# Two streamed attentions on one core: TensorE's products with V in halves around its waits, prompt scores and half of the sample scores further ahead in the second layer

## What is computed

```python
# first layer, 8 heads with two maps each
s = jnp.einsum('bqhcd,bkhcd->bhcqk', qb, kb).astype(jnp.float32) * scale
p = jax.nn.softmax(jnp.where(mask, s, -jnp.inf), axis=-1)
w = p[:, :, 0] - lam * p[:, :, 1]
outs.append(jnp.einsum('bhqk,bkhd->bqhd', w.astype(v.dtype), vb))
...
# second layer, 16 heads
z = jnp.einsum('bqhd,bkhd->bhqk', qb, kb).astype(jnp.float32) * scale
log_1m = jnp.where(mask, jax.nn.log_sigmoid(-z), 0.0)
suffix = lax.cumsum(log_1m, axis=3, reverse=True) - log_1m
a = jnp.where(mask, jnp.exp(jax.nn.log_sigmoid(z) + suffix), 0.0)
outs.append(jnp.einsum('bhqk,bkhd->bqhd', a.astype(v.dtype), vb))
```

## Time and profile before

| | |
|---|---|
| median of 3 runs | 1731.0 us (1729.71 to 1731.71) |
| profiled execution, its own time | 1729.45 us |
| its span | 1727.7 us |
| busy: TensorE (PE) | 1672.1 us, 97% |
| busy: VectorE (DVE) | 1148.0 us, 66% |
| busy: ScalarE (ACT) | 755.9 us, 44% |
| first attention, about | 195 to 375 us of the span |
| second attention, about | 1045 to 1240 us |
| mean granted clock of TensorE | 0.997 |

### The profile page before, as it was taken

The page is one execution under the profiler, slowest core; times in us unless marked ns, Lnnn a source line. Parts: engine busy times, 40 slices in busy tenths (PEclk is TensorE's granted clock), DMA queues, the critical chain, the costliest instruction groups (busy, mean ns, idle before and its releaser), DMA issues.

```text
span 1727.7 us, 33287 instructions
## 1 busy us (share of the span) xinstructions
PE 1672.1 (97%) x14036; PEld 1546.4 (90%) x14036; DVE 1148.0 (66%) x1587; ACT 755.9 (44%) x1272; POOL 160.8 (9%) x155
## 2 busy tenths in 40 slices
PE   7999999999999999999999999999999999999999
PEld 7999765679999999999999996666799999999999
DVE  6663366666996598478742326777779946984884
ACT  5443355564543245134442214666555522541341
POOL 0000100002221011001000000000032100110120
PEclk9999999999999999999999999999999999999999
DMA  5135699942223122212223247999312221222222
GB/s 183 68 104 210 258 384 373 374 190 74 74 76 121 50 74 98 98 50 98 98 84 128 107 170 307 379 366 380 120 50 86 86 98 50 98 98 74 74 92 93
DMA packets 38751, 258.74 MB, mean 150 GB/s; under 512 B 4560, under 2 KB 4944, under 8 KB 9552
## 3 DMA queue, kind: packets, MB, share of 16 engines
q1 hardware_dynamic: 34848, 245.15, 38.2%
q0 software_dynamic: 3760, 11.54, 1.9%
HBM read 242.51 MB, written 13.11 MB: 148 GB/s over the span
## 4 chain that ended last, share of the span: by engine, by line
PE 86%; DVE 8%; ACT 3%; issue 2%; DMA 0%; SPq 0%; ACTq 0%; DVEq 0%
PE ps L784 29%; PE ps L564 28%; PE ps L265 4%; PE ps L266 4%; PE ps L267 4%; PE ps L1242 3%; PE ps L1142 2%; PE ps L1191 2%; PE ps L600 2%; PE ps L1158 2%; PE ps L1171 1%; PE ps L1146 1%; DVE s_lo L733 1%; PE ps L1213 1%; DVE pw L1509 1%
## 5 line engine op out<-in xcount | busy, mean ns | idle before, releaser
L265 PE MATMUL ps<-w_hi,h_hi 128*128 128x256 f32 x640 | 182.9, 286 | 11.4 <-DVE h_lo L297 10.3
L243 DVE TENSOR_TENSOR w_lo<-w_raw,w_hi 128x2048 fp32r<-128x2048 f32 x55 | 126.0, 2291 | 88.2 <-ACT w_hi L227 79.4
L266 PE MATMUL ps<-w_lo,h_hi 128*128 128x256 f32 x640 | 181.8, 284 | 0.0
L267 PE MATMUL ps<-w_hi,h_lo 128*128 128x256 f32 x640 | 181.7, 284 | 0.0
L729 ACT ACTIVATE s_hi<-t 128x512 fp32r<-128x512 f32 x176 | 109.5, 626 | 155.3 <-PE ps L784 76.6
L227 ACT ACTIVATE w_hi<-w_raw 128x2048 fp32r<-128x2048 f32 x54 | 103.1, 1910 | 165.6 <-PE ps L564 158.0
L784 PE MATMUL ps<-hs_hi,s_hi 128*128 128x320 f32 x528 | 163.8, 310 | 0.0
L784 PE MATMUL ps<-hs_hi,s_lo 128*128 128x320 f32 x528 | 163.1, 309 | 0.0
L784 PE MATMUL ps<-hs_lo,s_hi 128*128 128x320 f32 x528 | 163.1, 309 | 0.0
L564 PE MATMUL ps<-gu_hi,w_hi 128*128 128x320 f32 x692 | 158.0, 309 | 0.2
L564 PE MATMUL ps<-gu_lo,w_hi 128*128 128x320 f32 x692 | 157.6, 309 | 0.0
(11 more groups left out here) (253 smaller groups left out, 4140.1 us busy)
## 6 DMA issues: line engine op xcount, KB each, us to landing
w_raw<-in_w SPq DMA_DIRECT2D x99, 1024.0 KB, 4.8
kv<-in_k_s SPq DMA_DIRECT2D x30, 1024.0 KB, 7.9
kv<-in_v_a SPq DMA_DIRECT2D x18, 1024.0 KB, 8.3
work<-in_v_s SPq DMA_DIRECT2D x16, 1024.0 KB, 8.6
kv<-in_k_a SPq DMA_DIRECT2D x14, 1024.0 KB, 8.5
work<-in_v_a SPq DMA_DIRECT2D x14, 1024.0 KB, 9.1
extra<-in_k_a SPq DMA_DIRECT2D x8, 1024.0 KB, 7.5
w_raw<-in_k_a SPq DMA_DIRECT2D x8, 1024.0 KB, 9.1
```

The costliest lines, as they stand in the source:

```text
L243: nc.vector.tensor_tensor(w_lo[s][:, :, :], w_raw[:, s, :, :], w_hi[s][:, :, :].bitcast(F32), ALU.subtract).then_inc(lo_done, 1)
L265: nc.tensor.matmul(out, s_hi, m_hi, start=first, stop=False, skip_group_check=True)
L266: nc.tensor.matmul(out, s_hi, m_lo, start=False, stop=False, skip_group_check=True)
L267: return nc.tensor.matmul(out, s_lo, m_hi, start=False, stop=last, skip_group_check=True)
```

## The change

Three edits, all in TensorE's order. `pe_s` and `pe_v` get a parameter `part`, which lets a caller issue the first half (waits and all) and the second half (with the new tokens' part) apart. In the first attention `pe_v(n - 1)` is cut: its first half goes ahead of `pe_pv(k)`, its second stays between `pe_w1` and `pe_w2`. In the second attention `pe_ps(k + 1)` goes ahead of `pe_pt(k, 0)`; the first half of `pe_v(n - 1)` goes ahead of `pe_pt(k, 1)`, and the first half of `pe_s(n + 1)` ahead of `pe_pt(k + 1, 1)`.

```diff
-            def pe_s(self, n):
+            def pe_s(self, n, part=range(2)):
...
-                pe.wait_ge(s["q"], self.queries(n))
-                self.wait(pe, s["x"], n)
+                if 0 in part:
+                    pe.wait_ge(s["q"], self.queries(n))
+                    self.wait(pe, s["x"], n)
...
-                for h in range(2):
+                for h in part:
...
+                if 1 not in part:
+                    return
...
-            def pe_v(self, n):
+            def pe_v(self, n, part=range(2)):
...
-                pe.wait_ge(s["wn"], n + 1)
-                pe.wait_ge(s["wne"], n + 1)
-                self.wait(pe, s["o"], n)
+                if 0 in part:
+                    pe.wait_ge(s["wn"], n + 1)
+                    pe.wait_ge(s["wne"], n + 1)
+                    self.wait(pe, s["o"], n)
...
-                for h in range(2):
+                for h in part:
...
+                if 1 not in part:
+                    return
...
                     self.pe_pt(k, 0)
                     self.pe_ps(k + 1)
+                    if n > 0:
+                        self.pe_v(n - 1, [0])
                     self.pe_pv(k)
                     self.pe_w1(n)
                     if n > 0:
-                        self.pe_v(n - 1)
+                        self.pe_v(n - 1, [1])
                     self.pe_w2(n)
...
                     k = 2 * n
+                    self.pe_ps(k + 1)
                     self.pe_pt(k, 0)
-                    self.pe_ps(k + 1)
+                    if n > 0:
+                        self.pe_v(n - 1, [0])
                     if len(self.blocks(k, 1)):
                         self.pe_pt(k, 1)
                     if n > 0:
-                        self.pe_v(n - 1)
+                        self.pe_v(n - 1, [1])
                     self.pe_pv(k)
...
                     self.pe_pt(k + 1, 0)
                     self.pe_w2(n)
+                    if n + 1 < N_PAIRS:
+                        self.pe_s(n + 1, [0])
                     if len(self.blocks(k + 1, 1)):
                         self.pe_pt(k + 1, 1)
                     if n + 1 < N_PAIRS:
-                        self.pe_s(n + 1)
+                        self.pe_s(n + 1, [1])
                     self.pe_pv(k + 1)
```

## The result

| | before | after |
|---|---|---|
| median | 1730.36 us (4 runs, 1729.04 to 1731.71) | 1717.8 us (4 runs, 1717.16 to 1719.39) |
| profiled execution's span | 1727.7 us | 1716.3 us |
| TensorE busy | 1672.1 us | 1674.4 us |

The ratio is 0.9932, with a 95% interval of 0.992 to 0.9945; by the medians it is 12.6 us less. The same kernel measured once more beside the last experiments gave 1718.75 us against 1729.36, a ratio of 0.9937 (0.9924 to 0.9951).

What follows compares the result with a forecast made beforehand. TensorE's idle time in the two attentions, about 16 and 15 us at most, was the field. Gains of 9 (first attention) and 1 (second) made -10 us: 1721 from a 1731.0 median, range 1713.5 to 1727.5.

Steps and rivals of the forecast that it cites:

- The signs named in advance: First-attention pair at 21 us, exponential waits under 4, second attention's pair about as before, its 6.6 us VectorE wait staying.
- (1): First attention, slots 1 to 15: half the V product fills TensorE's idle time before the transposes; 9 us gained.
- The cost of the shapes: Each piece set apart on TensorE costs 0.26 us: 0.15 entering the other tile shape, 0.11 leaving it.
- rival 5: No change: every shape switch costs a whole matmul, 0.27 us, 0.54 a pair; 1729.5 us, chance 0.07.
- The next wait in line, L1225: First attention: L1225 needs ScalarE's copy, no slack in odd slots; 0.3 late in all 15 gives back 4.5 us.
- (2): Second attention, prompt's next scores ahead of transposes: one shape alternation less, 0.13 us in 8 even slots, 1 us.
- rival 4: Slower: second attention's transposes, moved behind the scores, come late for ScalarE's queue and VectorE; 1736 us, chance 0.05.
- (3): Second attention, halves of sample scores and V ahead of second transposes: fills 0.25 us, pays 0.26; nothing gained.
- The second attention together: All second-attention edits gain 1 us, with bounds of +3 and -8.
- rival 3: Second attention is bound by TensorE after all and gains 8 us; 1714 us, chance 0.08.
- Transfers: First attention's K and V loads, at DMA share 0.99, are not yet a limit: 13 us of lead against 9 lost.
- Clock: Low-clock stretch at the second attention's start, 6.8 us, costs at most 3.4 us; 0 counted, 3.4 kept either way.

Runs made afterwards that it cites:

- the first attention alone: Kernel before with only the first attention's edit, half of V ahead of the prompt's product; 1718.56 us, ratio 0.9942.
- three variants: Changed kernel with V's leading half cut again (1720.47 us), whole V ahead (1723.98), or odd slots' V half behind earlier sample scores plus two second-attention moves (1720.48).
- the scores alone: Kernel before with only the second attention's next prompt scores moved ahead of the transposes; 1729.91 us, ratio 1.0.
- second alone: Kernel before with only the second attention's edits, first attention in its old order; 1727.13 us, ratio 0.9993.

## Why the prediction was right

1721 was predicted, between 1713.5 and 1727.5; 1717.8 was measured, 12.6 us less than before where 10 was said. The signs named in advance came too: the pair of the first attention at 20.84, its wait on the exponential at 0.8 in all, the second attention shorter by less than 3. Only the 6.6 us on VectorE did not stay whole, 4.5 are left.

- **(1) V's half in the first attention: right, and the term a little small.** 9 was taken between 8.1 and 10.0; the first attention alone gave 10.3 at full clock and 10.5 by the medians, above both. The even slot gained 0.94 us (255.61 to 265.21 is 9.60, 256.26 to 266.80 was 10.54) where 0.70 to 0.885 was said, the odd one 0.63 (244.37 to 255.61 is 11.24, 266.80 to 278.67 was 11.87) where 0.54 to 0.64. Two readings were too cautious. The idle time was taken from the brackets, which count from the modelled end of a matmul. By the starts the odd slot stood idle for 0.85 us (see the result) and not 0.80, and 0.85 - 0.22 is the 0.63. And the bound of 0.885 was passed, because four transposes behind a wait take 0.59 us to the next piece and without one 0.53 (255.61 to 256.14).
- **The cost of the shapes: right in size.** 0.15 + 0.11 = 0.26 was read from the rows, 0.22 is what the new rows show. The 0.15 is too high by these 0.06, since the transposes it was read from stood behind a wait and those they were compared with did not: 0.53 - 0.44 = 0.09. A change of tiling, which by the Trainium skill (TensorEngine Tiling (Array Packing), Key Properties) drains TensorE by a time that it does not give, costs about that much here and not a matmul's 0.27 on each side: rival 5 fell with it.
- **The next wait in line, L1225 (now L1228): right.** "No slack left" in odd slots is 0.2 us. It did not open in the change and opened in each of the three variants that delayed the copy or took its cover away: 1.4, 7.1 and 10.4 us, without the 0.7 of slot 0 that the kernel before has too.
- **(2) Scores ahead: small, as said, but not by what was said.** 0.13 us a pair was predicted for the shape switch in the even slot, 0.05 measured. TensorE is still the later there, 1136.48 against VectorE's end at 1135.65 + 0.69 = 1136.34. The delay of the transposes was covered and rival 4 fell: with the scores alone the time was that of before, 1729.91 against 1729.08.
- **(3) The halves: wrong in which part gains.** "Fills 0.25 and pays 0.26: nothing" came out as 0.18 a pair. The filled time was larger than the bracket: it ran from the end of the four transposes, about 1136.63 + 0.44 at their quick pace (the row of 1136.63 stands above), to 1137.49, so 0.4 and not 0.25, and 0.4 less the 0.22 of the shapes is 0.18. It counts because the pair waits for these scores, through ScalarE's sigmoid and VectorE's scan, whose wait went from 2.35 to 2.17; the prediction had not followed that chain. That the other piece, V's half, brings nothing was right as far as it was run, in the old order of the prompt's scores.
- **The second attention together:** 1 predicted; 1.6 to 1.8 by the lengths at equal clock, with its own bound of +3 to -8. That the sum came near is in part luck: it was put down to the scores ahead, which bring 0.05 a pair, and most of it came from the half that was to bring nothing. TensorE's idle time does not decide there, as read from the earlier trace rows, and rival 3 (8 us) fell.
- **Transfers: right.** 13 us of lead was more than needed, and with a quarter fewer bytes the time is the same. What the Trainium skill (DMA: Bandwidth & Descriptors, Where 436 GB/s comes from) gives as memory's limit for a core, about 358 GB/s, was passed by 405 here with one core at work.
- **Clock: 0 counted, 3.4 kept open.** Of the two profiles, the one after lost 1.3 us by it in the first attention and won 0.9 in the second.

The sum by parts at equal clock is 10.3 and 1.6 to 1.8, so about 12, within the interval of the ratio (9.5 to 13.8 us). Compared over all runs of like mean clock it is a little less: at 0.997 the kernel before took 1729.62 us (mean of 21 runs) and the change 1718.46 (5), at 0.998 1728.70 (8) and 1717.61 (2), so 11.1 to 11.2. The rest of the 12.6 between the medians of four runs may be clock and chance.

## What to carry to other kernels

Where an engine is busy 91% of a stage and waits once or twice in each pass, look for which of its own pieces stand ahead of the start of the chain it later waits for. A piece moved from there into the wait is worth what it fills, up to about its length, less what its changes of shape cost (0.885 us of work gave 0.94 and 0.63 here), as long as every wait in the pass keeps its own cover. Here one block covered one wait, two waits wanted two pieces, and a third piece lost. Before moving anything ahead of a producer, follow what the producer feeds, on every in-order queue: eight saved pairs of switches of 0.22 us cost 7 us that way. And where two profiles differ by a few microseconds, compare stage lengths at equal clock before giving the difference to the edit.

## What the runs showed of the hardware

- A DMA share of 1.01 at 405 GB/s was no sign of a bound here: 308 GB/s with a share of 0.85 ran in the same time.
- Going from full 128 x 128 tiles to 32-column tiles and back costs TensorE about 0.22 us (0.09 on the way in, 0.13 on the way out), at matmuls of 0.055 us each. A further piece put between transposes and the prompt's scores (64 x 128 tiles) cost 0.13.
- Four transposes take 0.06 to 0.07 us longer to the next piece when TensorE waited just before them: 0.59 (256.26 to 256.85) against 0.53 (255.61 to 256.14) in the first attention, 0.50 (1125.86 to 1126.36) against 0.43 (1136.48 to 1136.91) in the second.
- At the start of an attention, after some microseconds of scattered work, the granted clock fell to the lower level for 3.4 or 6.8 us in some profiles and not in others, with the same order of instructions up to there. From 195 to 205 us TensorE was busy for 7.35 us in a profile without it (the kernel before) and for 7.41 in one with it (second alone). It cost 1.3 us for 3.4 and 1.8 for 6.8 in the first attention, so less than half of the stretch, probably because TensorE waited for others in part of it anyway.
